# The second attention's value products by pairs of heads with the values stationary, and a minimum as the exponential's bias

## What is computed

```python
def mla_attend(q_nope, q_pe, k_nope, k_pe, v, q_pos, k_pos):
    s = (jnp.einsum('bqhd,bkhd->bhqk', q_nope, k_nope, preferred_element_type=jnp.float32)
         + jnp.einsum('bqhr,bkr->bhqk', q_pe, k_pe, preferred_element_type=jnp.float32))
    s = s * ((MLA_NOPE_DIM + MLA_ROPE_DIM) ** -0.5)
    mask = (k_pos // CHUNK)[None, :] <= (q_pos // CHUNK)[:, None]
    p = jax.nn.softmax(jnp.where(mask, s, NEG_INF), axis=-1)
    return jnp.einsum('bhqk,bkhd->bqhd', p.astype(v.dtype), v)
```

## Time and profile before

| | us |
|---|---|
| median of 3 runs | 3655.07 (3654.46 to 3658.21) |
| the profiled execution | 3655.49 |
| its span | 3653.8 |
| TensorE busy | 3079.8 (84%) |
| VectorE busy | 2554.5 (70%) |
| ScalarE busy | 1204.6 (33%) |
| GpSimd busy | 1551.4 (42%) |
| mla_attend of the three groups | 45.2, 118.8, 167.4 |

### The profile page before, as it was taken

One profiled execution on the slowest core, in us unless ns is written; L12 is line 12 of the kernel. 1 busy time (PEld: TensorE's weight loads), 2 busy tenths in 40 slices (PEclk: granted clock), 3 DMA queues, 4 the chain that ended last, 5 costly groups with the idle time before them and its releaser, 6 DMA issues. The chain is left out here.

```text
span 3653.8 us, 36056 instructions
## 1 busy us (share of the span) xinstructions
PE 3079.8 (84%) x10134; PEld 1743.5 (48%) x10134; DVE 2554.5 (70%) x5090; ACT 1204.6 (33%) x3180; POOL 1551.4 (42%) x1184
## 2 busy tenths in 40 slices
PE   8979999676869897767876888999988999899977
PEld 5755755334535454435643545444444444444433
DVE  0132069878577878878847757888888887788884
ACT  0231234654433436754622413222222222222211
POOL 0000035657553278877563783333333333243330
PEclk9979999785889998886778989999999999999989
DMA  4665589566679998576487989999999999999993
GB/s 139 237 221 171 175 320 397 191 184 213 221 227 385 333 342 260 152 206 205 142 274 266 366 272 394 409 403 401 406 406 408 401 399 398 379 405 394 407 395 116
DMA packets 374424, 1097.69 MB, mean 300 GB/s; under 512 B 90800, under 2 KB 208720, under 8 KB 288080
## 3 DMA queue, kind: packets, MB, share of 16 engines
q0 software_dynamic: 165072, 751.05, 55.5%
q1 hardware_dynamic: 175312, 303.04, 23.8%
q10 hardware_dynamic: 33840, 41.30, 3.2%
HBM read 1031.16 MB, written 63.02 MB: 299 GB/s over the span
## 5 line engine op out<-in xcount | busy, mean ns | idle before, releaser
L429 POOL DMA_INDIRECT expert_rows<-in_experts,picked_index x640 | 770.5, 1204 | 1326.2 <-DVE ff_sum L584 1177.6
L572 DVE SCALAR_TENSOR_TENSOR expert_rows<-expert_rows,h_tile 128x1024 f32<-128x1024 f32 x672 | 818.9, 1219 | 208.1 <-DMA expert_rows<-in_experts,picked_index 191.9
L584 DVE SCALAR_TENSOR_TENSOR ff_sum<-expert_rows,coefficients,ff_sum 128x1024 f32<-128x1024 f32 x672 | 860.6, 1281 | 107.5 <-ACT coefficients L535 106.4
L1795 PE MATMUL dense_act_ps<-dense_hT,key_columns 128*128 128x384 f32 x2048 | 724.2, 511 | 139.8 <-DMA key_columns<-in_key_columns 100.2
L452 POOL DMA_INDIRECT gates_by_expert<-dense_gate,gate_address x384 | 673.1, 1753 | 163.0 <-issue 128.8
L1803 PE MATMUL dense_out_ps<-dense_value_rows,dense_weights 128*128 128x512 f32 x1536 | 687.0, 599 | 23.7 <-DVE dense_weights L1869 23.7
L1795 PEld LDWEIGHTS dense_act_ps<-dense_hT,key_columns 128*128 128x128 f32 x2048 | 401.1, 199 | 478.9 <-DMA key_columns<-in_key_columns 161.7
L1803 PEld LDWEIGHTS dense_out_ps<-dense_value_rows,dense_weights 128*128 128x128 f32 x1536 | 294.5, 192 | 377.0 <-issue 318.2
L833 PE MATMUL proj_ps<-xT,w_in_block 128*128 128x384 f32 (+1 forms) x1392 | 422.6, 467 | 36.8 <-PEq L1608 16.0
L833 PEld LDWEIGHTS proj_ps<-xT,w_in_block 128*128 128x128 f32 x1392 | 267.7, 193 | 190.9 <-issue 37.8
L529 ACT ACTIVATE activated<-dots 128x1 f32<-128x1 f32 (+1 forms) x634 | 125.3, 198 | 585.3 <-DVE expert_rows L572 568.3
(11 more groups left out here) (183 smaller groups left out, 3169.9 us busy)
## 6 DMA issues: line engine op xcount, KB each, us to landing
key_columns<-in_key_columns SPq DMA_DIRECT2D x128, 512.0 KB, 11.5
dense_value_rows<-in_experts SPq DMA_DIRECT2D x128, 512.0 KB, 8.4
gates_by_expert<-zeros POOLq DMA_DIRECT2D x12, 2048.0 KB, 22.2
wq_half<-in_peer_wq SPq DMA_DIRECT2D x48, 512.0 KB, 11.6
dense_gates<-gates_by_expert SPq DMA_DIRECT2D x128, 192.0 KB, 10.3
w_in_block<-in_w_in ACTq DMA_DIRECT2D x18, 1024.0 KB, 9.7
w_in_block<-in_w_in SPq DMA_DIRECT2D x18, 1024.0 KB, 8.5
w_out<-in_w_out SPq DMA_DIRECT2D x3, 4096.0 KB, 17.3
```

The lines of the kernel that those rows point to most:

```text
L429: pool.indirect_dma_start(to, None, self.a["experts"], bass.IndirectOffsetOnAxis(ap=index[:, k:k + 1], axis=0)).then_inc(self.got[p % self ...
L572: dve.scalar_tensor_tensor(place, place, 1.0, self.h[n % 2][:], ALU.mult, ALU.mult, accum_out=self.dots[:, s % TOPK:s % TOPK + 1]).then_in ...
L584: dve.scalar_tensor_tensor(total, self.ring[:, p % self.RING, D:2 * D], self.coef[:, y % TOPK:y % TOPK + 1], total, ALU.mult, ALU.add).the ...
L1795: mm = nc.tensor.matmul(up[it % 2][:, 0:W], keys[it % KB][:, k, :], hTd[:, k, :], start=(k == 0), stop=(k == KC - 1))
```

## The change

In mla_project the gains of the queries are multiplied by minus the softmax scale, so that scores arrive negated and scaled. In mla_attend the row minimum of the negated scores is the bias itself, and the exponential takes scale -1; the masked corner is filled with the opposite sign. Value products are issued for two heads at once, every second turn, with the values as stationary operand and the turned probabilities as moving one; the sums come out with head dimensions on partitions, even heads on the lower 64 and odd heads on the upper 64, in two PSUM banks. The turned probabilities have three buffers instead of two. The inverse row sums of a tile are transposed by TensorE into 8 partitions, copied by ScalarE, and spread over 64 partitions a head by eight matmuls whose stationary operand picks one head. ScalarE copies the sums to mla_outT, and VectorE multiplies them there by the spread inverses, one turn later than its copy was.

```diff
@@ mla_project, VectorE
             dve.wait_ge(g_in, 16)
+            nc.vector.tensor_scalar(gain[:, 0:QC], gain[:, 0:QC], -MLA_SCALE, None, ALU.mult).then_inc(gain_scaled, 1)
+            dve.wait_ge(gain_scaled, 1)
@@ mla_attend, buffers
-        pT = [mem.at(f"probsT{i0 + i}", FG + 69632 + 4096 * i, [P, 1024]) for i in range(2)]
-        on = [mem.at(f"mla_out{i0 + i}", FG + 77824 + 2048 * i, [P, SBW]) for i in range(2)]
-        mx = mem.at(f"row_max{g.n}", FG + 81920, [P, N])
+        pT = [mem.at(f"probsT{3 * g.n + i}", FG + 69632 + 4096 * i, [P, 1024]) for i in range(3)]
+        riT = [mem.at(f"inverse_sumT{i0 + i}", FG + 98176 + 512 * i, [P, P]) for i in range(2)]
-        op = s.enter_context(nc.psum_tensor(f"mla_out_ps{g.n}", [P, 512], F32))
-        oT = s.enter_context(nc.psum_tensor(f"mla_outT_ps{g.n}", [P, 512], F32))
+        op = banks(nc, s, f"mla_out_ps{g.n}_", 2)
+        half = [slice(HD * par, HD * par + HD) for par in range(2)]
@@ TensorE
                 n = t - 2
-                if 0 <= n < N:
+                if 0 <= n < N and n % 2:
                     i, h = items[n]
                     pe.wait_ge(t_copied, n + 1)
-                    if h == 0 and turn(i) >= 1:
-                        pe.wait_ge(on_done, turn(i))
+                    if h == 1 and turn(i) >= 1:
+                        pe.wait_ge(on_done, 2 * turn(i))
                     for x, (off, rows, vt) in enumerate(tiles):
-                        mm = nc.tensor.matmul(op[0:r, HD * h:HD * (h + 1)], pT[n % 2][0:rows, P * x:P * x + r],
-                                              f["mv"][0:rows, vt, HD * h:HD * (h + 1)], ...)
+                        for par in range(2):
+                            first = HD * (h - 1 + par)
+                            mm = nc.tensor.matmul(op[par][half[par], P * (h // 2):P * (h // 2) + r], f["mv"][0:rows, vt, first:first + HD],
+                                                  pT[(n - 1 + par) % 3][0:rows, P * x:P * x + r], ...)
                     mm.then_inc(av_done, 1)
+                    if h == HEADS - 1:
+                        pe.wait_ge(inv_done, turn(i) + 1)
+                        nc.tensor.transpose(op[1][0:HEADS, 0:r], ri[0:r, HEADS * turn(i):HEADS * (turn(i) + 1)], m["ident"][0:r, 0:r]).then_inc(riT_done, 1)
                 n = t - 3
                 if 0 <= n < N and items[n][1] == HEADS - 1:
-                    pe.wait_ge(on_done, turn(i) + 1)
-                    if turn(i) >= 1:
-                        pe.wait_ge(oT_copied, turn(i))
+                    pe.wait_ge(riT_copied, turn(i) + 1)
                     for x in range(4):
-                        mm = nc.tensor.transpose(oT[:, P * x:P * x + r], on[turn(i) % 2][0:r, P * x:P * (x + 1)], m["ident"][0:r, 0:r])
-                    mm.then_inc(oT_done, 1)
+                        for par in range(2):
+                            pick = m["ident"][0:HEADS, 2 * x + par:2 * x + par + 1].broadcast_to([HEADS, HD])
+                            mm = nc.tensor.matmul(op[1 - par][half[par], P * x:P * x + r], pick, riT[turn(i) % 2][0:HEADS, 0:r], ...)
+                    mm.then_inc(spread, 1)
@@ ScalarE
-            for t in range(N + 1):
+            for t in range(N + 3):
                     nc.scalar.activation(p[t % 2][0:r, 0:nk], sp[t % 2][0:r, 0:nk], ACT.Exp, bias=nm[0:r, t:t + 1],
-                                         scale=MLA_SCALE, accum_out=rs[0:r, t:t + 1]).then_inc(p_done, 1)
+                                         scale=-1.0, accum_out=rs[0:r, t:t + 1]).then_inc(p_done, 1)
...
-                    if n >= 2:
-                        act.wait_ge(av_done, n - 1)
+                    if n >= 3:
+                        act.wait_ge(av_done, (n - 3) // 2 + 1)
...
+                n = t - 3
+                if 0 <= n < N and items[n][1] == HEADS - 1:
+                    act.wait_ge(riT_done, turn(i) + 1)
+                    nc.scalar.copy(riT[turn(i) % 2][0:HEADS, 0:r], op[1][0:HEADS, 0:r]).then_inc(riT_copied, 1)
+                    for par in range(2):
+                        nc.scalar.copy(f["obT"][half[par], :, g.at[i]:g.at[i] + r],
+                                       op[par][half[par], :].rearrange("p (x q) -> p x q", x=4)[:, :, 0:r]).then_inc(o_copied, 1)
-                bg.act((n + 1) / N)
+                bg.act(min(1.0, t / N))
@@ VectorE
-                        nc.vector.memset(sp[t % 2][0:CHUNK, nk - CHUNK:nk], FAR).then_inc(masked, 1)
+                        nc.vector.memset(sp[t % 2][0:CHUNK, nk - CHUNK:nk], -FAR).then_inc(masked, 1)
-                    nc.vector.reduce_max(mx[0:r, t:t + 1], sp[t % 2][0:r, 0:nk], AX).then_inc(max_done, 1)
-                    dve.wait_ge(max_done, t + 1)
-                    nc.vector.tensor_scalar(nm[0:r, t:t + 1], mx[0:r, t:t + 1], -MLA_SCALE, None, ALU.mult).then_inc(nm_done, 1)
+                    nc.vector.tensor_reduce(nm[0:r, t:t + 1], sp[t % 2][0:r, 0:nk], AX, ALU.min).then_inc(nm_done, 1)
                 n = t - 2
-                    dve.wait_ge(av_done, n + 1)
                     dve.wait_ge(p_done, n + 1)
                     nc.vector.reciprocal(ri[0:r, at], rs[0:r, at]).then_inc(inv_done, 1)
-                    dve.wait_ge(inv_done, turn(i) + 1)
-                    nc.vector.tensor_tensor(on[turn(i) % 2][0:r, :]..., op[0:r, :]..., ri[0:r, at]..., ALU.mult).then_inc(on_done, 1)
-                n = t - 3
+                n = t - 4
-                    dve.wait_ge(oT_done, turn(i) + 1)
-                    nc.vector.tensor_copy(f["obT"][:, :, g.at[i]:g.at[i] + r], oT[:]...).then_inc(oT_copied, 1)
+                    dve.wait_ge(spread, turn(i) + 1)
+                    for par in range(2):
+                        own = f["obT"][half[par], :, g.at[i]:g.at[i] + r]
+                        dve.wait_ge(o_copied, 2 * turn(i) + par + 1)
+                        nc.vector.tensor_tensor(own, own, op[1 - par][half[par], :]..., ALU.mult).then_inc(on_done, 1)
```

More of the change, by code:

```diff
@@ L1310, in _ @@
                     r = rows_of(i)
-                    pe.wait_ge(on_done, turn(i) + 1)
-                    if turn(i) >= 1:
-                        pe.wait_ge(oT_copied, turn(i))
+                    pe.wait_ge(riT_copied, turn(i) + 1)
                     for x in range(4):
-                        mm = nc.tensor.transpose(oT[:, P * x:P * x + r], on[turn(i) % 2][0:r, P * x:P * (x + 1)], m["ident"][0:r, 0:r])
-                    mm.then_inc(oT_done, 1)
+                        for par in range(2):
+                            pick = m["ident"][0:HEADS, 2 * x + par:2 * x + par + 1].broadcast_to([HEADS, HD])
+                            mm = nc.tensor.matmul(op[1 - par][half[par], P * x:P * x + r], pick, riT[turn(i) % 2][0:HEADS, 0:r],
+                                                  start=True, stop=True, skip_group_check=True)
+                    mm.then_inc(spread, 1)
         @block.scalar
         def _(act):
-            for t in range(N + 1):
+            for t in range(N + 3):
                 if t < N:
@@ L1336, in _ @@
                     act.wait_ge(t_done, n + 1)
-                    if n >= 2:
-                        act.wait_ge(av_done, n - 1)
+                    if n >= 3:
+                        act.wait_ge(av_done, (n - 3) // 2 + 1)
                     if i < TILES:
-                        nc.scalar.copy(pT[n % 2][:, 0:P * len(tiles)], tp[:, 0:P * len(tiles)]).then_inc(t_copied, 1)
+                        nc.scalar.copy(pT[n % 3][:, 0:P * len(tiles)], tp[:, 0:P * len(tiles)]).then_inc(t_copied, 1)
                     else:
-                        nc.scalar.copy(pT[n % 2][0:NEW, 0:r], tp[0:NEW, 0:r])
+                        nc.scalar.copy(pT[n % 3][0:NEW, 0:r], tp[0:NEW, 0:r])
                         for x in (1, 2):
-                            ins = nc.scalar.copy(pT[n % 2][:, P * x:P * x + r], tp[:, P * x:P * x + r])
+                            ins = nc.scalar.copy(pT[n % 3][:, P * x:P * x + r], tp[:, P * x:P * x + r])
                             if x == 2:
                                 ins.then_inc(t_copied, 1)
-                bg.act((n + 1) / N)
+                n = t - 3
+                if 0 <= n < N and items[n][1] == HEADS - 1:
+                    i = items[n][0]
+                    r = rows_of(i)
+                    act.wait_ge(riT_done, turn(i) + 1)
[4 more added lines that the diff above has]
+                bg.act(min(1.0, t / N))
         @block.vector
@@ L1351, in _ @@
             cut = 0
-            for t in range(N + 3):
+            for t in range(N + 4):
                 if t < N:
@@ L1380, in _ @@
                     r = rows_of(i)
-                    dve.wait_ge(oT_done, turn(i) + 1)
-                    nc.vector.tensor_copy(f["obT"][:, :, g.at[i]:g.at[i] + r],
-                                          oT[:].rearrange("p (x q) -> p x q", x=4)[:, :, 0:r]).then_inc(oT_copied, 1)
+                    dve.wait_ge(spread, turn(i) + 1)
+                    for par in range(2):
```

(4 more changed lines are left out.)

28 lines of the change are left out of this document (12 added, 16 removed).

## The result

The changed kernel takes 3675.18 us (median of 7 executions, 3665.21 to 3679.24); the kernel before, on the same chip, 3654.58 (7 executions). The ratio is 1.0053, with a 95% interval of 1.0042 to 1.0064: slower by 0.53%, some 19 us, where I had put 0.24 on slower and 3647 us as the time. The range of 3622 to 3672 does not hold it.

What follows compares the result with a forecast made beforehand. Neither TensorE, mostly at its lower clock, nor VectorE was taken to fill the second-attention stages; waits between engines bound them. Stages +3, -1, -10 us gave -8 and 3647 us; 8-in-10 range 3622 to 3672, the forecast's own 3637 to 3656.

Steps and rivals of the forecast that it cites:

- -2 -2 +7 = +3: First stage, us: -2 shorter value products, -2 the minimum, +7 net for new waits at tile ends.
- Rival A: Second attention: granted clock rises with the new value products; stages -2, -6, -16 us, together 3631; chance 0.15.
- The ends: First stage's tile ends: new waits 5.2 and 3.8 us, old stalls 1.5 and 0.8, net 7 us.
- The new waits: Each tile's end: TensorE waits for the inverse, the inverse sums' copy, then VectorE's products; +7, +7, +8.5 us by stage.
- the second end: Second stage's second tile end: background between reductions at 932.82 and 940.85 outlasts the chain, so about 1 us.
- hand-over (1): At each tile's end TensorE waits for the inverse, behind VectorE's reduction two heads after the tile's last.
- Minimum: 72 small VectorE operations go, 0.13 us each: -3.1 us in second and third stage, -2 in first.
- Pairs: Paired value products: shorter score waits -2.6 and -10 us, old stalls -3.2 and -5.4, second and third stage.
- the old stalls: VectorE's waits for value sums two heads after a tile, removed: 3.2 and 5.4 us, second and third stage.
- D: Rival: the two halves don't overlap, value products stay at 0.204, -10 and -2.6 fall away: 3660; chance 0.05.
- B: Rival: tile ends decide, six at full 4 to 6 us; stages +5, +6, -2, together +9, 3664; chance 0.23.
- C: Rival for the whole kernel: nothing arrives, gains and stalls cancel, 3655 us; chance 0.15.

Runs made afterwards that it cites:

- e10: First group with old second attention and minimum, others paired with tile-end steps moved; plus eight unread VectorE reductions at the first group's first tile end; ratio 1.0015.
- e11: Kernel before with the minimum; pairs of heads, tile-end steps moved later, in the third group only; 3645.27 us, ratio 0.9977.
- e3: Changed kernel without the scaling by inverse sums (inverse transpose, its copy, spreading and VectorE's two products left out); 3645.36 us, ratio 0.9972.
- e2: Changed kernel, but the first group of tiles uses the second attention of before, with the minimum; 3659.11 us, ratio 0.9999.
- e5: The changed kernel itself once more, unaltered, beside the kernel before; ratio 1.0052.
- e1: Kernel before with the minimum as bias only (gains turned and scaled, 72 small VectorE operations fewer); 3651.61 us, ratio 0.999.
- e9: The kernel before itself, profiled once more unaltered; profiled execution 3661.36 us.
- e4: Changed kernel with tile-end transpose, spreading and products each one turn later, next value products waiting for ScalarE's copies only; 3655.93 us, ratio 0.9999.
- e8: Changed kernel, instruction order kept; next tile's value products wait for ScalarE's two copies, not VectorE's products; 3660.51 us, ratio 1.0023.
- e7: Changed kernel plus one unread 128-column matrix product in every TensorE turn of the first group's second attention; ratio 1.0059.

## Why the prediction was wrong, step by step

**The first stage, the main error.** I summed -2 -2 +7 = +3; it was +15.6 (of the first profiles alone, 14.9). Three steps failed. *The clock was a constant in the sum.* I took it from the earlier trace rows as 0.73 for the stage, an average of a lower and an upper part, and priced waits at their length. e10 shows a stall of 3 us there to cost 12. Rival A let the clock follow upwards; that it could be lost in the first stage, where it had come up between 255 and 260 us, I had not considered. The Trainium skill (TensorE: Matmul & The Clock Gate, Part 1: The HAM clock gate) says that the slow level is the default and that activity releases it. The slices above agree in part: in before and in e11 the upper level comes behind a busy stretch at 0.50. But in e10 TensorE is busy 10.00 of 10 us twice in a row, as the profile counts it, and the clock stays at 0.50, so the rule as it stands does not give this case. It would still have been the rival to write down. How much of the 15.6 us is clock and how much waits the runs do not separate. *The value products* were to save 2 us: the pairs alone (e3) cost 7.8, or 2.2 to 7.8 by the profile compared with. For short heads the rhythm is worse even at one clock. In the first tile, both kernels at the lower level, reductions of every second head start 3.1 us apart after:

```profile
243.08 0.29 DVE L1377 TENSOR_REDUCE minus_max<-score_ps 128x1 f32<-128x128 f32 x1
...
244.16 0.45 PE L1293 MATMUL probsT_ps<-identity,probs 128*128 128x128 f32 x1 [0.67 <-ACT probsT L1346]
...
246.19 0.29 DVE L1377 TENSOR_REDUCE minus_max<-score_ps 128x1 f32<-128x128 f32 x1
```

and 2.6 us apart with the minimum alone's code (e2):

```profile
243.74 0.45 PE L1293 MATMUL probsT_ps<-identity,probs 128*128 128x128 f32 x1
...
243.96 0.29 DVE L1363 TENSOR_REDUCE minus_max<-score_ps 128x1 f32<-128x128 f32 x1
...
244.31 0.74 PE L1282 MATMUL score_ps<-mla_kT,mla_qT 96*128 96x128 f32 x2
...
246.57 0.29 DVE L1363 TENSOR_REDUCE minus_max<-score_ps 128x1 f32<-128x128 f32 x1
```

With both heads' value products in one turn, the other turn has none to cover the head's softmax, and TensorE waits 0.67 us for ScalarE's copy once a pair. TensorE's own time did not fall either: from the transpose at 244.16 through the pair's four value records to the next scores at 245.16 it takes 1.00 us, and the other head's transpose 0.22 more (245.75 to 245.97), together 1.22; two single heads take 0.57 each with their transposes (243.74 to 244.31 in e2), together 1.14. Here a value record of before cost 0.165 us (243.98 to 244.31 for two), not the 0.204 that I took from long heads. The weights of those scores are loaded after a gap that the single heads' rows don't have:

```profile
245.16 0.50 PEld L1282 LDWEIGHTS score_ps<-mla_kT,mla_qT 96*128 96x128 f32 x2 [0.33 <-issue]
```

I had counted records, not what covers what. *The ends* were 7 and measured 10.1 (e3 against after), with the clock's share in it.

**The new waits, mechanism right, two sizes wrong.** For the second stage's first end I had put the reductions for e+3, e+4 and e+5 6.6 and 6.4 us apart (898.70, 905.3, 911.7); after has:

```profile
909.51 0.69 DVE L1377 TENSOR_REDUCE minus_max<-score_ps 128x1 f32<-128x512 f32 x1
...
915.88 0.69 DVE L1377 TENSOR_REDUCE minus_max<-score_ps 128x1 f32<-128x512 f32 x1
...
922.23 0.69 DVE L1377 TENSOR_REDUCE minus_max<-score_ps 128x1 f32<-128x512 f32 x1
```

6.37 and 6.35: the chain and its prices hold. The step that failed is the second end, to which I gave 1 us because VectorE's background "fills the time". It was 8.03 and 3.87 us from reduction to reduction before (932.82, 940.85, and 944.72), and is 10.59 and 7.34 after:

```profile
945.74 0.82 DVE L1377 TENSOR_REDUCE minus_max<-score_ps 128x1 f32<-128x640 f32 x1
...
948.75 1.28 ACT L376 ACT_TABLE_LOAD   x1
...
950.04 0.79 ACT L1335 ACTIVATE probs<-score_ps,minus_max 128x640 f32<-128x640 f32 x1
...
951.70 1.97 PE L1320 MATMUL mla_out_ps<-inverse_sumT,identity 8*64 8x128 f32 x16 [5.64 <-ACT inverse_sumT L1358]
...
956.18 0.11 DVE L1374 MEMSET score_ps<- 64x64 f32 x1 [4.54 <-PE score_ps L1282]
```

The minimum ends at 946.6, but the exponential starts at 950.04: ScalarE is in its own background, busy without a break from 944.25 on, with two changes of the function table of 1.28 us each. The small copy is queued behind that exponential, the spreading behind the copy, and the next scores behind the spreading. (In before the same batch stands there too, but the exponential starts 2.5 us after the reduction began, at 935.31, and after 4.3.) So ScalarE's background lengthens the first interval instead of covering it. In the second, 3.5 us longer than before, VectorE waits 2.2 us for scores that stand behind the hand-over for its products. Together 6 us where I had 1. In the third stage hand-over (1), which I had left without a price, was the longest of TensorE's waits for a hand-over, 7.3 us:

```profile
1741.74 1.53 PE L1305 MATMUL mla_out_ps<-probsT,mla_v 128*64 128x128 f32 x24
1750.59 0.37 PE L1311 MATMUL mla_out_ps<-identity,inverse_sum 128*8 128x128 f32 x1 [7.32 <-DVE inverse_sum L1384]
```

The cause: VectorE came late to its reduction and inverse, after 4.2 us of waiting for gathered rows (4.2 us for this hand-over in e5 as well). Together +11.9 and +13.8 where I had 8.5 and 8.2.

**The second and third stage otherwise.** Minimum: -5.0 and -1.3 against -3.1 each, the sum right within the scatter. Pairs: -7.6 and -13.6 (e3 against e1) against -5.8 and -15.4. In the traces these were right, the old stalls' removal included, though the whole time shows only part of it. Value products cost what the earlier trace rows said: 24 records in 1.53 us at 1741.74, 0.064 each, the spreading 1.97 us at the lower clock. So D is out.

**The clock in the third stage.** I said that 0.80 would prove me wrong, and it came (0.75 in e5). But before itself has 0.75 in e9, and there 14 us less of TensorE's time made the stage only 3.2 us shorter. 0.66 was one execution. The test that I had set up could not tell my forecast from A. TensorE's time was not what most of the third stage waited for in either clock.

**The rivals.** B had the right mechanism and sign, with 3664 against 3675. Its ends and tail come to 15.2 and 16.5 us in the second and third stage, where 13.8 and 11.9 were measured. Its nearness to the total is partly luck: the second stage was +6 for a measured +1.2, the first +5 for +15.6, and what it lacked there is the clock and the pairs' own loss. It deserved more than 0.23: I had worked out its chain in numbers for one end and then let an assumed cover discount the others. C and A did not happen.

**What stays open.** The stages explain 13.8 us of the 19. The stretches between the first and second stage do not differ; the others scatter between executions (behind the third stage 1811.0 us in e9, 1819.0 in after, 1831.0 in e4, though the three run the same code there), so two profiles of each kernel can't place the remaining 5 us. Open too are what decides when the clock comes up, and its share in the first stage's loss.

## What to carry to other kernels

Ask of every stage in which the clock comes up late whether the change adds idle time ahead of the rise: there a wait can cost several times its length (four times in e10), and the shortest stage can decide. When an operation is placed in an engine's order behind another engine's small copy, follow that copy through everything queued ahead of it on its own engine, background and function tables included; cover on one engine is no cover on the other. And let a consumer wait for what frees its own part of a buffer (here ScalarE's copies), not for the last user of the other part: in e8 that was worth 0.3%. And set a gain read off the stages beside the time of the whole: here they differ by up to 12 us.

## What the runs showed of the hardware

- One stall of about 3 us on VectorE, of which TensorE idled 1.36, and the granted clock stayed at its lower level for the following 30 us and more (e10; the clock is read in one execution, the loss shows in the median of ten), although TensorE was then busy 9.33, 10.00 and 10.00 of every 10 us; without the stall it came up in that place (e11). Added work did raise it in e7. More than this about when it rises the runs don't show.
- The granted clock of one and the same stage differs between executions: 0.64 and 0.77 (47.8 and 42.2 us) in the first, 0.66 and 0.75 in the third. A clock read off a single profile is not a property of the kernel.
- Waits of 3.3 us in all, taken away, made the first stage 7.2 us shorter in one profile (e8).
- At the lower clock the weight load of scores behind value records or the spreading starts 0.33 us after the load before it ended (at 245.16, 248.27, 257.09 and 261.48 in after). From a head's transpose to its value records it is 0.38 us on 64 columns (244.16 to 244.54) and 0.24 on the whole array (243.74 to 243.98 in e2), so that switch costs 0.14 us; the 0.1 of the earlier trace rows was read at the upper clock.
